# Hybrid mLSTM / RWKV-7 / PEER block: four changes of order, in the one-hots and in the expert values

## The reference

```
q = xn @ w_query;  s = q . sub_keys          # 8 heads, two halves, 128 keys each
idx, gate = top 16 of 256 sums per head      # gate: softmax of the 16 best
act = gelu(sum_d xn[d] * expert_u[idx][d])   # 128 experts per token
out = sum_e (gate * act)[e] * expert_v[e]
```

## Time and profile before

| | before |
|---|---|
| median of 3 runs | 4357.12 us |
| profiled execution | 4364.53 us, span 4362.8 us |
| TensorE busy | 4054.5 us, 93% of the span |
| VectorE, ScalarE, GpSimd busy | 2577.8, 1518.1, 2306.3 us |
| gates stage, first 12 units | 2301 to 2491 us of the span |
| gates stage, other 64 units | 2491 to 3069 us |
| values stage | 3178 to 4338 us |

### The profile page before, as it was taken

How to read it: one execution, slowest core, us unless ns; L and a number is a source line. 1 busy time by engine, 2 the same in 40 slices (tenths; PEclk the granted TensorE clock), 3 DMA queues, 4 the chain that set the end, 5 groups by cost and what they waited for, 6 DMA issues and landing times.

```text
span 4362.8 us, 70174 instructions
## 1 busy us (share of the span) xinstructions
PE 4054.5 (93%) x27233; PEld 3590.8 (82%) x27233; DVE 2577.8 (59%) x3407; ACT 1518.1 (35%) x2053; POOL 2306.3 (53%) x930
## 2 busy tenths in 40 slices
PE   7999999999999999899996799999989888988897
PEld 5777777777787778799996688889988888888887
DVE  4344443444544541577753566666458888888785
ACT  4333322333322211333335566666322222222223
POOL 5322222323244344355553466666677778777774
PEclk9999999999999999999999999999999999999998
DMA  3222222222222442333344599999898889898793
GB/s 119 96 85 81 85 76 93 83 83 85 95 99 96 151 159 96 133 129 128 127 144 168 218 361 365 359 362 365 319 361 328 336 333 353 336 345 339 292 341 121
DMA packets 258397, 899.44 MB, mean 206 GB/s; under 512 B 107672, under 2 KB 140696, under 8 KB 162736
## 3 DMA queue, kind: packets, MB, share of 16 engines
q1 hardware_dynamic: 175984, 482.50, 31.3%
q0 software_dynamic: 46080, 335.56, 18.8%
q10 hardware_dynamic: 36160, 78.85, 4.7%
HBM read 828.10 MB, written 68.71 MB: 206 GB/s over the span
## 4 chain that ended last, share of the span: by engine, by line
PE 61%; issue 14%; DVE 10%; ACT 5%; POOL 4%; DMA 3%; SPq 2%; ACTq 1%; POOLq 0%; DVEq 0%
PE ps L389 14%; PE ps L391 13%; PE ps L390 13%; PE ps L1984 4%; PE ps L1986 4%; PE ps L1985 4%; POOL wl L384 4%; DVE ps L1482 3%; PE ps L1674 2%; DMA raw<-stream 2%; DVE gal L1486 2%; ACT oh L1033 2%; SPq L555 1%; ACT wh L380 1%; DVE stage L1470 1%
## 5 line engine op out<-in xcount | busy, mean ns | idle before, releaser
L384 POOL TENSOR_TENSOR wl<-raw,wh 128x2048 fp32r<-128x2048 f32 x396 | 1835.0, 4634 | 1924.6 <-ACT wh L380 1924.6
L389 PE MATMUL ps<-xh,wh 128*128 128x352 f32 (+1 forms) x3904 | 1437.7, 368 | 37.9 <-DVE xl L1162 18.9
L391 PE MATMUL ps<-xh,wl 128*128 128x352 f32 (+1 forms) x3904 | 1403.6, 360 | 0.0
L390 PE MATMUL ps<-xl,wh 128*128 128x352 f32 (+1 forms) x3904 | 1403.0, 359 | 0.0
L380 ACT ACTIVATE wh<-raw 128x2048 fp32r<-128x2048 f32 x396 | 758.3, 1915 | 1528.3 <-PE ps L391 667.1
L389 PEld LDWEIGHTS ps<-xh,wh 128*128 128x128 f32 x3904 | 742.7, 190 | 134.5 <-issue 44.8
L391 PEld LDWEIGHTS ps<-xh,wl 128*128 128x128 f32 x3904 | 741.9, 190 | 83.3
L390 PEld LDWEIGHTS ps<-xl,wh 128*128 128x128 f32 x3904 | 743.2, 190 | 81.4 <-issue 7.7
L1984 PE MATMUL ps<-gah,wh 128*128 128x352 f32 x2048 | 687.3, 336 | 115.7 <-DVE H L1498 86.3
L1986 PE MATMUL ps<-gah,wl 128*128 128x352 f32 x2048 | 677.4, 331 | 0.0
L1985 PE MATMUL ps<-gal,wh 128*128 128x352 f32 x2048 | 676.4, 330 | 0.0
(11 more groups left out here) (333 smaller groups left out, 3959.0 us busy)
## 6 DMA issues: line engine op xcount, KB each, us to landing
raw<-stream SPq DMA_DIRECT2D x396, 1024.0 KB
gelu_scratch<-preb ACTq DMA_DIRECT2D x128, 176.0 KB
gates_scratch<-stage ACTq DMA_DIRECT2D x22, 1024.0 KB
gt<-gates_scratch SPq DMA_DIRECT2D x32, 704.0 KB
act<-gelu_scratch SPq DMA_DIRECT2D x32, 704.0 KB
mergegate_scratch<-sgb ACTq DMA_DIRECT2D x32, 256.0 KB, 2.1
sgm<-mergegate_scratch SPq DMA_DIRECT2D x32, 256.0 KB, 2.7
h_in<-x_t SPq DMA_DIRECT2D x4, 1024.0 KB, 8.5
```

The source lines that it names most:

```text
L384: pool.tensor_tensor(wl[s][:, :], raw[s][:, :], wh[s][:, :].bitcast(F32), ALU.subtract).then_inc(w_lo, 1)
L389: pe.matmul(dst, w_h, h[:, kx, lo:], start=start, stop=False)
L390: pe.matmul(dst, w_h, l[:, kx, lo:], start=False, stop=False)
L391: return pe.matmul(dst, w_l, h[:, kx, lo:], start=False, stop=stop)
```

## The change

Four edits, all of order. (1) In the gates stage `onehots` is made one group further ahead: onehots(k+2) behind dense(2k+1) in place of onehots(k+1) behind dense(2k), with a second one before the loop. (2) On GpSimd `gated` stands in front of unit k's residual and fetches in place of behind them. (3) On ScalarE the wait for `w_used` and the rounding of unit k+2 stand in front of `act_halves`. (4) On VectorE a unit begins with its first use; then rows 0, rows 1, the other uses, dve_low, rows 2, rows 3. No instruction is added or taken away in total.

```diff
--- before.py
+++ after.py
@@ -682,14 +682,14 @@
 
             for k in range(NC4 * GROUPS):
                 g, c = divmod(k, NC4)
+                if g < GROUPS - 1:
+                    for e in (AHEAD if g else AHEAD_1)[c]:
+                        gated(g + 1, 1 - g % 2, e)
                 split_lo(pool, U_PEER + k, c % 2)
                 if k == 1:
                     pool.wait_ge(w_used, U_PEER)
                 for n in FETCHED[F_ALL + k]:
                     fetch(n)
-                if g < GROUPS - 1:
-                    for e in (AHEAD if g else AHEAD_1)[c]:
-                        gated(g + 1, 1 - g % 2, e)
             pool.wait_ge(rstd_ready, 1)
             for d in POOL_OUT:
                 pool.tensor_tensor(H[:, d, :], H[:, d, :], rstd3[:, :], ALU.mult).then_inc(scaled[1], 1)
@@ -1084,10 +1084,10 @@
             def act_values(g, s, ahead=AHEAD):
                 for c in range(NC4):
                     n = U_PEER + NC4 * g + c
+                    act.wait_ge(w_used, n + 1)
+                    split_hi(act, n + 2, c % 2)
                     for e in ahead[c]:
                         act_halves(g + 1, 1 - s, e)
-                    act.wait_ge(w_used, n + 1)
-                    split_hi(act, n + 2, c % 2)
 
             for s in range(2):
                 act_values(s, s, AHEAD_1 if s == 0 else AHEAD)
@@ -1502,19 +1502,20 @@
                 for c in range(NC4):
                     k = NC4 * g + c
                     fetched = USED[F_ALL + k]
+                    for n in fetched[:1]:
+                        use(n)
                     dve_rows(g, c, 0)
                     dve_rows(g, c, 1)
-                    for n in fetched[:1]:
-                        use(n)
-                    dve_rows(g, c, 2)
                     for n in fetched[1:]:
                         use(n)
                     for e in (AHEAD if g else AHEAD_1)[c]:
                         dve_low(g + 1, 1 - g % 2, e)
+                    dve_rows(g, c, 2)
                     dve_rows(g, c, 3)
 
 
             onehots(0)
+            onehots(1)
             for c in range(4):
                 dve.wait_ge(h_moved[c], 48)
             dve.tensor_tensor(xd, xh[:, :, 0:P].bitcast(F32), xl[:, :, 0:P].bitcast(F32), ALU.add).then_inc(sets_ready, 1)
@@ -1524,11 +1525,11 @@
                 used = list(USED[j])
                 for k in range(2 * j, 2 * j + 2) if j < GATES_TWO else range(GATES_TWO + j, GATES_TWO + j + 1):
                     dense(2 * k)
-                    if k + 1 < N // OH:
-                        onehots(k + 1)
                     if used and (j >= GATES_TWO or k % 2):
                         use(used.pop(0))
                     dense(2 * k + 1)
+                    if k + 2 < N // OH:
+                        onehots(k + 2)
                 for n in used:
                     use(n)
             for r in range(F_REST):
```

## The result

The changed kernel takes 4695.35 us, the median of 4 runs (4688.65 to 4700.82), against 4358.88 in the same comparison: ratio 1.0774, 95% interval 1.0753 to 1.0795. The forecast was 4626 us with a range of 4500 to 4690: the right way and most of the size, but 69 us short and 5 us over the range's end. The profiled execution took 4693.52 us, with a span of 4691.8, 329.0 above the span before.

The account below looks back on a forecast made before the run. TensorE, busy 93% of the span, was taken as the bound. Values stage 975 + 396 + 120 + 5 = 1496 against 1160, 336 more, less 67; 4364.5 + 269 - 7.4 = 4626 us, range 4500 to 4690.

Parts of the forecast that it names:

- The chain to rows 2: Values stage: rows 2 hang on unit k's end through rounding, gah, dve_low; 92 TensorE stops of 4.15 or 4.58 us, 396 us.
- S + 0.45: Values stage: ScalarE's rounding begins 0.45 us after S, the start of TensorE's unit, and takes 1.92 us.
- The lock: Values stage: GpSimd's residual holds VectorE's two-SBUF-input dve_low, asked for 0.4 us behind its start, until 0.39 us after its end.
- The first rival: At c = 0, dve_low gets served between gated and residual, so 30 units don't stop: 98 us less, 4528; chance 0.08.
- The clock: Values stage: low clock behind each of 92 new stops costs 1.3 us, 120 us in all, bounds 74 and 156.
- the forecast's own account of its 185 us: Old values stage beyond 975 us of undisturbed units: some 113 us idle time and some 58 us half-speed clock.
- +269: Whole kernel: values stage 336 us more, less 67 us saved by edit 1, gives 269 us more.
- Edit 1: Gates stage: saves 47 us in the first 12 units and 20 in the other 64, 67 in all (35 to 83).
- Traffic: Rival: memory traffic binds the 64 gates units, so edit 1 gives only 47 us, total 4646; no separate chance.
- dve_low in front of the residual everywhere: Values stage rival: dve_low always precedes the residual, stops and slow clock shrink, 197 us less with edit 1, 4160; chance 0.08.
- No change in the values stage: Rival: VectorE's order doesn't matter where it is far ahead, only edit 1 shows, total 4290; chance 0.04.
- Edit 2: GpSimd, values stage: gated in front of the residual; its waits for the group's DMAs were put at no cost.

Follow-up runs that it names:

- e12: The changed kernel with 24 extra matmuls that compute nothing behind the second quarter of units c = 0 to 2 in the values stage: 4707.55 us, ratio 1.0791.
- e4: The changed kernel with L1486 subtracting unwritten PSUM columns in place of gah, so one SBUF input and no low part computed: 4333.31 us, ratio 0.9922.
- e9: The changed kernel without edit 2, gated again behind the residual and the fetches: 4719.10 us, ratio 1.0817.
- e8: The kernel before with edit 1, and dve_low behind rows 3 of its unit in place of in front: 4269.64 us, ratio 0.9797.
- e10: The kernel before with edit 1, and upper(2k) before the previous unit's rounding and GELU in three of four of the last 64 gates units: 4286.26 us, ratio 0.9839.
- e2: The changed kernel without edit 3, act_halves again in front of the wait for w_used and the rounding: 4311.93 us, ratio 0.9902.
- e3: The changed kernel without edit 4, rows 2 in front of dve_low and the first use behind rows 1, as before: 4412.13 us, ratio 1.0122.
- e1: The kernel before with edit 1 alone: 4315.56 us, ratio 0.9903.

## Why the prediction came out as it did

**The chain to rows 2: right in its mechanism, the stops 7% too long.** The forecast had 92 stops of 4.15 or 4.58 us, 396 us in all. Measured are 91 on L1498, 355.7 us. An idle time counts from the modelled end of a matmul (0.32 us, where the next would start after 0.16), so from slot to slot a stop is 0.16 us longer: 4.07 us in the mean, 370 us in all. Half of the difference is S + 0.45 for the rounding, which is S + 0.34 (median of 87 units). The forecast took 1.91 us for a quarter that followed a restart, and the first quarter behind a restart takes 2.02 us (median of 50 in e12). The residual's 4.53 in place of 4.62 us is most of the rest. The other waits of the stage were 27 us, not 5, so the sum of all idle time, 397 us (1542 less 1160, and 0.16 for each of some 95) against 396 + 5, fits so closely by luck.

**The lock: right.** L1486 has a median of 4.58 us (the earlier trace rows shows one of 5.79), and with one input from SBUF none is over 0.52. The Trainium skill (SBUF — State Buffer, Who interferes with whom) names just this, two SBUF inputs on VectorE against a GpSimd instruction that reads SBUF, and e4 agrees. One sentence of the forecast was too strong: the second dve_low of the earlier trace rows starts 0.02 us behind the residual of the earlier trace rows and gets by, right behind the first.

**The first rival: near, and its condition never arose.** At c = 0 GpSimd does start the residual right behind a gated product, in 15 of 29 units, but only 0.15 to 0.37 us behind the rounding's end, and dve_low starts 0.04 us or more behind it in every one. The closest is this (GpSimd, then VectorE):

```profile
3435.62 0.96 POOL L669 TENSOR_TENSOR act<-act,gt 128x352 f32<-128x352 f32 x1
3436.53 4.52 POOL L384 TENSOR_TENSOR wl<-raw,wh 128x2048 fp32r<-128x2048 f32 x1
```

```profile
3436.57 4.87 DVE L1486 TENSOR_TENSOR gal<-act,gah 128x352 fp32r<-128x352 f32 x1 [3.50 <-ACT gah L1068]
```

So the changed kernel doesn't test it. e9 does: dve_low came first in 15 units of c = 0, with a gated product running, and waited for both. By the rule of the same page of the Trainium skill, that issue order decides, it would have gone before the residual; here the trace doesn't agree. Before the change 15 of 16 such waited as well. But it isn't a rule without exception: in e8, 5 of 22 got by in 0.57 to 0.63 us, all asked for in the last 0.2 us before the residual. That the rival failed is thus shown; that its condition was missed by 0.04 us is luck.

**The clock: the step that failed.** The forecast's term was 1.3 us for each stop, 120 us, with the reason that part of the slow stretch falls inside the longer stop. It doesn't. Over the 89 stops of 3.5 to 5 us the trace's clock is low for only 0.19 us inside a stop on average; the stretch begins from 1.6 us before the restart to 1.5 us behind it and falls almost whole into work, just as it did behind the shorter stops. The 24 matmuls behind these 89 restarts take 5.52 us in the mean, where 24 undisturbed ones take 3.85: 1.67 us lost, about as before the change (5.57 us, 14 stops). In the regular units the sum gives it too: 13.22 - 7.62 - 3.93 (3.77 + 0.16) = 1.67. Of this 0.11 is the restart itself and some 1.55 the low clock. For 92 stops it is 154 us, 34 more than forecast.

The stage has 1542 - 975 - 397 = 170 us beside idle time, 50 above the term of 120. The other 16 are no price of a stop. Some 14 of them the kernel before has as well: the forecast's own account of its 185 us, 113 idle and 58 clock, left 14 without a name, and the sum started from 975 without them. What they are stays open. So of the 63 us between the forecast's +269 and the +332 of the stages, 34 are the price of a stop, 16 this rest, 15 edit 1, and the chain is 4 the other way, with 2 between the stages. The median lies 69 us off and not 63 or 60, mostly as the forecast took 7.4 us off for its profiled execution, and the new one lay 1.8 under its median.

**Edit 1: right in the first 12 units (43 against 47 us), too large in the others (9 against 20).** I moved the stop from dense(2k+1) and didn't ask what was late next on the same engine. It was dense(2k): ScalarE now keeps up with TensorE, so its rounding, GELU and store issue come right at the start of a unit and hold upper(2k). After the change TensorE still waits for it 59 times and 30.6 us. e10 takes 41 of the 59 stops away, though only 7 us of their sum. Traffic, which I had named, was not yet the bound.

**The other rivals.** dve_low in front of the residual everywhere: no. No change in the values stage: no, and e2 and e3 show that only edits 3 and 4 together make the large loss. Edit 2 was priced at nothing and gains some 24 us (e9), since it takes the gated products out of the residual's way.

## What to carry to other kernels

When a reorder makes A wait for B, follow the whole chain from the event that B hangs on to the engine that sets the pace, and add what else holds each link (here the lock between VectorE and GpSimd, 4.6 us); here each link came within 0.12 us. Then price the clock for itself: in every trace the low clock came with each stop of 3.5 us and more, and in the changed kernel 1.67 us of work time were lost behind such a stop, so one of 4 us cost 5.7. And before booking the gain of a wait removed, look for the next one on the same engine and in the loads: from e1 to e2 TensorE's stops on VectorE fell from 81.6 to 6.2 us, and the time did not move.

## What was not expected of the hardware

- VectorE's two-input instruction is mostly kept out over two GpSimd instructions in a row, though it was there before the second (5.72 us at 3442.30 in e9; 15 of 16 before the change, 17 of 22 in e8).
- Matmuls that compute nothing, put into a stop, can pay for themselves in that unit: 2.7 us more work, and the unit 1.5 us shorter, as the clock stays at 2.4 GHz in it. No whole kernel with them was faster.
- Of the low stretch 0.09 us lay inside a stop of 2.7 to 3.2 us on average (14 stops before the change) and 0.19 inside one of 3.5 to 5 us (89 after it): the longer stop hardly swallowed more of it.
